# Loading the overflow flag before the last expert and closing a trunk kernel inside the branch

## The chip, the cores and the metric

The kernel runs on one core of one Trainium2 chip. The time is device microseconds of that core for one execution of the whole program. The four computing engines and the queues are called PE (matrix products; PEld is its weight load), DVE (vector), ACT (scalar activations), POOL (GpSimd) and SP (which issues the DMAs). Each runs its own instruction stream, and they meet only at semaphores.

## The reference, cut to what matters

Two layers over 256 tokens of width 1024 (4 tiles of 128x512 hold the residual stream). The part that this text is about is the second half of layer 1 and the last line:

```python
# layer 1: top-2-of-8 experts, each a SwiGLU of width 3584, then the final norm
logits = h @ w_router                       # 256 x 8
gates  = softmax(top2(logits))
for e in range(8):                          # only the tokens that chose e
    x[tok_e] += gate_e * ((silu(h[tok_e] @ w_gate[e]) * (h[tok_e] @ w_up[e])) @ w_down[e])
out = x * rsqrt(mean(x * x, axis=-1) + 1e-6) * final_norm
```

Layer 0 (dilated window attention and a dense SwiGLU) and the pooling mixer of layer 1 come before it and are the same in both kernels.

## The kernel before, in words

The tokens sit in `x` as two tiles `t` of 128 rows, each read in two column halves `n` of 512. Weights arrive from memory in units of 1 MB (128x2048 float32). ACT copies each unit to a rounded form `w_hi` (line 338), DVE subtracts it to get the rest `w_lo` (line 343), and PE forms three products per pair of operands (lines 375 to 377). At most three units are split ahead of PE, so ACT may split unit u+3 only when PE has finished unit u.

The experts run in a loop that each engine executes in its own stream: `Fori(0, 7)` holds seven experts, and the eighth, "the last expert", is written out once behind the loop, because it needs no next expert prepared. The tokens of an expert fit in 128 slots in the usual case. If one expert is chosen by more than 128 tokens, a second round over all eight experts is needed. Whether it is, stands in one integer in SBUF, `over_i` (the overflow flag), which DVE writes before the first expert. Each engine reads it into a register (`value_load`), compares and branches with `If(more != 0)`; behind it, in the usual case, an `Else` branch that is empty. The second round lies in the instruction stream between the branch and what follows.

Where the reading stands matters here. ACT and DVE first wait until the last piece of the last expert has been added to `x` (semaphore `x_added`, line 961 adds four pieces, in the order of `SCATTER`), then read the flag (lines 662 and 989), then branch (lines 663 and 990). Then the final norm: ACT sums the squares of tile 0 (line 475) and DVE those of tile 1 (line 681), DVE forms the mean (688), ACT the root (479), DVE the reciprocal (693), and DVE forms the four output pieces of 128x512 (line 1004). SP, which has read the flag and branched much earlier (lines 420, 421), stores each piece when it is ready (line 430) and waits until the stores have landed; then all engines meet in a closing barrier (line 154). PE reads and branches at lines 1343 and 1344.

Of the kernel before, what the change touches and what calls it, by code (L numbers as in the profile page):

```python
# [5 lines left out]
ALU = mybir.AluOpType  # L21
ACT = mybir.ActivationFunctionType
# [19 lines left out]
E = 8  # L42
# [106 lines left out]
def program(nc, x_in, ffn_norm, w_qkv, w_o, pool_w, pool_scale, w_gate, w_up, w_down,  # L149
# [4 lines left out]
    with ctx:  # L154
        def sb(name, shape, dt=F32, scope=ctx):
            return scope.enter_context(nc.sbuf_tensor(name, shape, dt))

        def sem(name):
            return ctx.enter_context(nc.semaphore(name))
# [28 lines left out]
        over_i = sb("over_i", [P, 1], I32)  # L188

# [94 lines left out]
        y_hi_ready, y_lo_ready = sem("y_hi_ready"), sem("y_lo_ready")  # L284
        scatter_ready, x_added, out_stored = sem("scatter_ready"), sem("x_added"), sem("out_stored")
# [100 lines left out]
        def _(sp):  # L386
# [34 lines left out]
            with sp.If(more != 0):  # L421
                with sp.Fori(0, E) as e:
                    expert(e + E, e)
            with sp.Else():
                sp.nop()
            for q in range(2 * TT):
                t, n = q // 2, q % 2
                cols = slice(n * 512, (n + 1) * 512)
                sp.wait_ge(hn_ready, TT + q + 1)
                sp.dma_start(out[t * P:(t + 1) * P, cols], hn[:, t, cols]).then_inc(out_stored, 16)  # L430
            sp.wait_ge(out_stored, 16 * 2 * TT)
# [35 lines left out]
        def _(act):  # L467
# [192 lines left out]
            round_of_experts(0)  # L660
            act.wait_ge(routed, 1)
            more = act.value_load(over_i[0:1, 0:1], min_val=0, max_val=1)
            with act.If(more != 0):
# [4 lines left out]
                act.nop()  # L668
            with act.Else():
                act.nop()  # L670
            squares(4)
            root(4)
# [3 lines left out]
        def _(dve):  # L676
# [289 lines left out]
            def round_of_experts(first):  # L966
# [10 lines left out]
                with dve.Fori(0, E - 1) as e:  # L977
                    expert(e + first, first, False)
                expert(first + E - 1, first, True)
                dve.wait_ge(x_added, START + 4 * (first + E))  # L980

# [6 lines left out]
            round_of_experts(0)  # L988
            more = dve.value_load(over_i[0:1, 0:1], min_val=0, max_val=1)
            with dve.If(more != 0):  # L990
# [4 lines left out]
                dve.nop()  # L995
            with dve.Else():
                dve.nop()
            squares(4)
            mean(4)
            invert(4)  # L1000
            for t in range(TT):
                for n in range(2):
                    cols = slice(n * 512, (n + 1) * 512)
                    nc.vector.scalar_tensor_tensor(hn[:, t, cols], x[:, t, cols], rstd(4, t), rows[:, 2, cols],
                                                   ALU.mult, ALU.mult).then_inc(hn_ready, 1)
# [406 lines left out]
```

## Time and profile before

| what | us |
|---|---|
| median of 3 runs | 1588.21 |
| lowest and highest | 1586.06 and 1589.52 |
| profiled execution: span | 1587.4 |
| busy: PE, DVE, ACT | 1540.5, 1233.1, 971.2 |
| last addition of the last expert ends | 1575.97 |
| first output piece starts | 1582.11 |

The profile is of one further execution; its own time is given by its span, from its first to its last instruction, and no figure is listed for what lies around the span. The span lies between the lowest and the highest of the runs. A busy share tells which engine carries the long stretches; the end of the program has to be read in the chain and the timeline, since nearly all engines are idle there.

### The profile page before, as it was taken

The page shows a single profiled execution, that of the slowest core. Times are in us where ns is not written, and L with a number is a line of the kernel's source. Part 1 is how long each engine was busy: PE and PEld are TensorE (multiplying, and loading weights), DVE is VectorE, ACT ScalarE, POOL GpSimd, SP SyncE. Part 2 cuts the span into 40 slices and gives each one's busy share as a digit, 9 for nine tenths or more (in the row PEclk, how much of TensorE's full clock was granted, in tenths as well). Part 3 has the DMA queues.
Part 4 walks back from the last instruction along what each step waited for, and adds up shares of the span by engine and source line. Part 5 has one row for each costly group of instructions (what it writes and reads, how often), then busy time and mean ns, then how long its engine had stood idle before and what let it go on. Part 6 is the DMA issues. An engine that isn't in the chain of part 4 may idle for free.

```text
span 1587.4 us, 22195 instructions
## 1 busy us (share of the span) xinstructions
PE 1540.5 (97%) x8546; PEld 1323.0 (83%) x8546; DVE 1233.1 (78%) x999; ACT 971.2 (61%) x797; POOL 89.9 (6%) x50
## 2 busy tenths in 40 slices
PE   6999999999999699999999999999999999999996
PEld 6999999899998688888888888888888888888885
DVE  6877667664445768888888888888888888888886
ACT  4344444454334457777777777777777777776774
POOL 1333223000000100000000000000000000000000
PEclk9999999999999689999999999999999999999998
DMA  9644443355557379999999999999999999999980
GB/s 310 201 146 133 134 153 127 94 186 186 183 182 246 132 264 341 355 342 342 361 340 358 338 347 362 337 360 336 339 358 347 334 359 345 341 362 341 357 301 28
DMA packets 217117, 436.80 MB, mean 275 GB/s; under 512 B 6992, under 2 KB 68176, under 8 KB 217056
## 3 DMA queue, kind: packets, MB, share of 16 engines
q1 hardware_dynamic: 215168, 432.11, 77.1%
q10 hardware_dynamic: 1552, 2.77, 0.5%
q0 software_dynamic: 336, 1.09, 0.2%
q8 instruction: 42, 0.69, 0.2%
q14 instruction: 19, 0.16, 0.0%
HBM read 434.88 MB, written 1.05 MB: 275 GB/s over the span
## 4 chain that ended last, share of the span: by engine, by line
PE 94%; DVE 4%; issue 1%; ACT 1%; DMA 0%; DVEq 0%; ACTq 0%; SPq 0%
PE bank L375 28%; PE bank L377 28%; PE bank L376 28%; PE bank L1249 2%; PE bank L1122 2%; PE bank L1259 2%; PE bank L1109 1%; PE bank L1099 1%; DVE w_lo L343 1%; DVE rot L764 1%; PE bank L1321 0%; PE bank L1322 0%; PE bank L1015 0%; DMA x<-in_x 0%; PE bank L1142 0%
## 5 line engine op out<-in xcount | busy, mean ns | idle before, releaser
L343 DVE TENSOR_TENSOR w_lo<-raw,w_hi 128x2048 fp32r<-128x2048 f32 x202 | 462.9, 2294 | 158.5 <-ACT w_hi L338 156.8
L338 ACT ACTIVATE w_hi<-raw 128x2048 fp32r<-128x2048 f32 x202 | 386.4, 1914 | 157.7 <-PE bank L377 154.6
L375 PE MATMUL bank<-w_hi,xg_hi 128*128 128x512 f32 x896 | 361.1, 403 | 0.0
L376 PE MATMUL bank<-w_lo,xg_hi 128*128 128x512 f32 x896 | 356.0, 397 | 0.0
L377 PE MATMUL bank<-w_hi,xg_lo 128*128 128x512 f32 x896 | 356.0, 397 | 0.0
L343 DVE TENSOR_TENSOR w_lo<-raw_late,w_hi 128x2048 fp32r<-128x2048 f32 x95 | 217.8, 2292 | 48.2 <-ACT w_hi L338 47.0
L343 DVE TENSOR_TENSOR w_lo<-raw_more,w_hi 128x2048 fp32r<-128x2048 f32 x96 | 220.0, 2291 | 29.6 <-ACT w_hi L338 28.9
L338 ACT ACTIVATE w_hi<-raw_more 128x2048 fp32r<-128x2048 f32 x96 | 184.0, 1917 | 55.7 <-PE bank L377 55.7
L377 PEld LDWEIGHTS bank<-w_hi,xg_lo 128*128 128x128 f32 x896 | 169.2, 189 | 41.3
L376 PEld LDWEIGHTS bank<-w_lo,xg_hi 128*128 128x128 f32 x896 | 169.7, 189 | 38.6
L375 PEld LDWEIGHTS bank<-w_hi,xg_hi 128*128 128x128 f32 x896 | 169.5, 189 | 38.7
L338 ACT ACTIVATE w_hi<-raw_late 128x2048 fp32r<-128x2048 f32 x95 | 181.7, 1913 | 31.9 <-PE bank L377 31.9
L375 PE MATMUL bank<-w_hi,a_hi 128*128 128x256 f32 (+1 forms) x592 | 174.2, 294 | 1.2 <-DVE rot L764 0.9
L377 PE MATMUL bank<-w_hi,a_lo 128*128 128x256 f32 (+1 forms) x592 | 171.0, 289 | 0.0
L376 PE MATMUL bank<-w_lo,a_hi 128*128 128x256 f32 (+1 forms) x592 | 170.9, 289 | 0.0
L375 PE MATMUL bank<-w_hi,hT_hi 128*128 128x512 f32 x384 | 152.8, 398 | 0.0
L376 PE MATMUL bank<-w_lo,hT_hi 128*128 128x512 f32 x384 | 152.2, 396 | 0.0
L377 PE MATMUL bank<-w_hi,hT_lo 128*128 128x512 f32 x384 | 152.2, 396 | 0.0
L375 PE MATMUL bank<-a_hi,w_hi 128*128 128x256 f32 x384 | 111.5, 290 | 5.7 <-DVE w_lo L343 5.7
L375 PEld LDWEIGHTS bank<-w_hi,a_hi 128*128 128x128 f32 x592 | 113.3, 191 | 3.7 <-issue 1.0
L377 PEld LDWEIGHTS bank<-w_hi,a_lo 128*128 128x128 f32 x592 | 113.4, 192 | 1.4
L376 PEld LDWEIGHTS bank<-w_lo,a_hi 128*128 128x128 f32 x592 | 113.5, 192 | 0.8
(158 smaller groups left out, 1991.0 us busy)
## 6 DMA issues: line engine op xcount, KB each, us to landing
raw_more<-in_moe_w_gate SPq DMA_DIRECT2D x48, 1024.0 KB, 5.5
raw<-in_moe_w_gate SPq DMA_DIRECT2D x48, 1024.0 KB, 5.4
raw_late<-in_moe_w_down SPq DMA_DIRECT2D x48, 1024.0 KB, 5.2
raw<-in_moe_w_up SPq DMA_DIRECT2D x40, 1024.0 KB, 5.5
raw_late<-in_moe_w_up SPq DMA_DIRECT2D x40, 1024.0 KB, 5.2
raw<-in_moe_w_down SPq DMA_DIRECT2D x40, 1024.0 KB, 5.1
raw<-in_attn_w_qkv SPq DMA_DIRECT2D x36, 1024.0 KB, 5.1
raw_more<-in_moe_w_up SPq DMA_DIRECT2D x32, 1024.0 KB, 5.7
```

Source lines behind the costliest of these rows:

```text
L338: nc.scalar.activation(w_hi[:, u % SPLIT, :], where, ACT.Copy).then_inc(hi_ready, 1)
L343: nc.vector.tensor_tensor(w_lo[:, u % SPLIT, :], home(u, i)[0], w_hi[:, u % SPLIT, :].bitcast(F32), ALU.subtract).then_inc(lo_ready, 1)
L375: nc.tensor.matmul(bank, hi, w[0], start=start, stop=False)
L376: nc.tensor.matmul(bank, hi, w[1], start=False, stop=False)
L377: return nc.tensor.matmul(bank, lo, w[0], start=False, stop=stop)
L764: last = nc.vector.tensor_tensor(turned[to:to + h2], bank[of:of + h2], sin[of:of + h2, :].unsqueeze(1).to_broadcast([h2, 2, SEQ]), ALU.mult)
L1099: last = nc.tensor.matmul(ps[3 + side][:, at:at + kn], qkT[part, c % 2, 0, g, pair, t * P:(t + 1) * P], qkT[part, c % 2, 1, g, pair, k0:k0 ...
L1109: last = nc.tensor.transpose(ps[5 + side][:, k * P:(k + 1) * P], e_sb[:, side, k * P:(k + 1) * P], ident[:, :])
L1122: last = nc.tensor.matmul(ps[7][:, side * HD:(side + 1) * HD], eT[:, side, k * P:(k + 1) * P], v_sb[:, c % 2, g, kt, col:col + HD], start= ...
L1249: last = nc.tensor.matmul(bank[:, q * P:(q + 1) * P], src[:, c:c + P], pick[:, t, :], start=t == 0, stop=t == TT - 1)
L1259: last = nc.tensor.transpose(ps[6][:, q * P:(q + 1) * P], h[:, q * P:(q + 1) * P], ident[:, :])
```

## The change

Three of the five streams change behind the loop of experts (PE only in the numbers of its lines; POOL not at all).

1. ACT and DVE read the overflow flag between the loop and the last expert. SP reads it where it did.
2. The comparison is turned round, `If(more == 0)`: the usual case is now the code directly behind the branch, and the second round is in the `Else`. The closing work (`finish`, and on SP `store_output`) is written out in both branches, so that in the usual case each of the three engines leaves the branch by a jump over the second round to the closing barrier.
3. The squares are all summed on ACT, in four pieces of 128x512, each as soon as its addition is done. The root-mean factor is formed from the four sums.
4. Tile 1 of the output is formed in two steps: DVE multiplies `x` by the gain row while ACT still sums squares, and ACT scales that by the reciprocal root. Tile 0 is formed by DVE as before. SP stores tile 0's two pieces, then tile 1's.

```diff
+            def store_output():
+                for t, ready in ((0, hn_ready), (1, out_ready)):
+                    for n in range(2):
+                        sp.wait_ge(ready, (TT if t == 0 else 0) + n + 1)
+                        sp.dma_start(out[t * P:(t + 1) * P, cols], hn[:, t, cols]).then_inc(out_stored, 16)
+                sp.wait_ge(out_stored, 16 * 2 * TT)
+
+            with sp.If(more == 0):
+                store_output()
+            with sp.Else():
                 with sp.Fori(0, E) as e:
                     expert(e + E, e)
-            with sp.Else():
-                sp.nop()
...
                 with act.Fori(0, E - 1) as e:
                     expert(e + first, False)
+                more = None
+                if not first:
+                    act.wait_ge(routed, 1)
+                    more = act.value_load(over_i[0:1, 0:1], min_val=0, max_val=1)
                 expert(first + E - 1, True)
                 load_table(ACT.Sqrt, 2 if first else 0)
-                act.wait_ge(x_added, START + 4 * (first + E))
...
+            def finish(first):                      # ACT
+                junk = (hn[:, 0, 0:512], sg[:, :], hn[:, 0, 512:D], h[:, :])
+                for q, (n, t, _bank) in enumerate(SCATTER):
+                    act.wait_ge(x_added, START + 4 * (first + E - 1) + q + 1)
+                    nc.scalar.activation(junk[q], x[:, t, n * 512:(n + 1) * 512], ACT.Square, scale=D ** -0.5,
+                                         accum_out=ssq[:, n, t:t + 1]).then_inc(ssq_ready, 1)
+                root(4)
+                act.wait_ge(rstd_ready, 5)
+                for n in range(2):
+                    act.wait_ge(weighted_ready, n + 1)
+                    nc.scalar.activation(hn[:, 1, cols], hn[:, 1, cols], ACT.Copy, scale=rstd(4, 1)).then_inc(out_ready, 1)
...
+            def finish(first):                      # DVE
                 dve.wait_ge(x_added, START + 4 * (first + E))
+                for n in range(2):
+                    nc.vector.tensor_tensor(hn[:, 1, cols], x[:, 1, cols], rows[:, 2, cols], ALU.mult).then_inc(weighted_ready, 1)
+                dve.wait_ge(ssq_ready, 4)
+                nc.vector.scalar_tensor_tensor(stat[:, 4, 2:2 + TT], ssq[:, 0, :], EPS, ssq[:, 1, :], ALU.add, ALU.add)
+                invert(4)
+                for n in range(2):
+                    nc.vector.scalar_tensor_tensor(hn[:, 0, cols], x[:, 0, cols], rstd(4, 0), rows[:, 2, cols],
+                                                   ALU.mult, ALU.mult).then_inc(hn_ready, 1)
```

What DVE holds from the last expert's additions on. Before, the flag's load and the branch follow the additions, and the second round (from the third row on from the branch) lies between the branch and the norm:

```order
499 L961 SCALAR_TENSOR_TENSOR x<-bank,gate_w,x 128x512 x4
500 L989 TENSOR_LOAD over_i
501 L989 ISA x2
502 L990 COMPARE_AND_BRANCH
503 L343 TENSOR_TENSOR w_lo<-raw_more,w_hi 128x2048 x3
...
677 L996 UNCONDITIONAL_BRANCH
678 L681 ISA hn,stat<-x 128x1024
679 L681 ISA stat 128x1
680 L688 TENSOR_SCALAR stat<-stat 128x2
681 L693 RECIPROCAL stat<-stat 128x2
682 L1004 SCALAR_TENSOR_TENSOR hn<-x,stat,rows 128x512 x4
```

The same place of DVE in the changed kernel, beginning with the loop's own branch (460):

```order
460 L981 COMPARE_AND_BRANCH
461 L986 TENSOR_LOAD over_i
462 L986 ISA x2
463 L330 TENSOR_TENSOR w_lo<-raw,w_hi 128x2048 x3
...
501 L965 SCALAR_TENSOR_TENSOR x<-bank,gate_w,x 128x512 x4
502 L1012 COMPARE_AND_BRANCH
503 L995 TENSOR_TENSOR hn<-x,rows 128x512 x2
504 L997 SCALAR_TENSOR_TENSOR stat<-ssq 128x2
505 L697 RECIPROCAL stat<-stat 128x2
506 L1002 SCALAR_TENSOR_TENSOR hn<-x,stat,rows 128x512 x2
507 L1012 UNCONDITIONAL_BRANCH
508 L330 TENSOR_TENSOR w_lo<-raw_more,w_hi 128x2048 x3
```

The load went from behind the additions to in front of the last expert's first own split; the norm stands directly behind the branch; and a jump (507) follows the norm, over the second round. ACT's stream changes in the same way.

SP around its branch and at its end, before; row 297 stores the four output pieces, row 298 waits for their landing:

```order
179 L420 TENSOR_LOAD over_i
180 L420 ISA x2
181 L421 COMPARE_AND_BRANCH
182 L422 UNCONDITIONAL_BRANCH
...
296 L424 UNCONDITIONAL_BRANCH
297 L430 DMA out<-hn 128x512 x4
298 L154 UNCONDITIONAL_BRANCH
```

SP now:

```order
181 L416 COMPARE_AND_BRANCH
182 L413 DMA out<-hn 128x512 x4
183 L416 UNCONDITIONAL_BRANCH
184 L419 UNCONDITIONAL_BRANCH
...
297 L413 DMA out<-hn 128x512 x4
298 L418 UNCONDITIONAL_BRANCH
```

The jump over the second round's DMAs stood ahead of the stores (181 to 297) and now stands behind them (183 to behind 298); it is row 183 that waits for the landing.

## Rows read from the trace of the kernel before

**Rows 1.** The page: span, busy time by engine, shares of the chain that ended last.
```profile
span 1587.4 us, 22195 instructions
PE 1540.5 (97%) x8546; PEld 1323.0 (83%) x8546; DVE 1233.1 (78%) x999; ACT 971.2 (61%) x797; POOL 89.9 (6%) x50
PE 94%; DVE 4%; issue 1%; ACT 1%; DMA 0%; DVEq 0%; ACTq 0%; SPq 0%
```

**Rows 2.** The chain in order of time from 1570: start us, us, what.
```profile
1573.24 2.74 DVE x L961 x4
1575.97 0.03 issue
1576.00 0.55 DVEq L989
...
1576.91 0.06 DVEq L990
1576.97 3.23 issue
1580.21 0.58 DVE hn L681
...
1582.11 0.75 DVE hn L1004
```

**Rows 3.** Lines 662, 663, 1344: durations ns min/median/max, first and last start.
```profile
L662 ACTq TENSOR_LOAD <-over_i x1: 488/488/488, 1576.0 to 1576.0; - x1
L663 ACTq COMPARE_BRANCH  x1: 54/54/54, 1576.8 to 1576.8; - x1
L1344 PEldq COMPARE_BRANCH  x1: 3654/3654/3654, 1574.0 to 1574.0; - x1
```

**Rows 4.** Timeline from 1576: start us, us, engine, instruction, [idle before].
```profile
1579.58 1.06 ACT L475 ACTIVATE hn<-x 128x1024 f32<-128x1024 f32 x1 [5.73 <-issue]
1581.47 0.17 DVE L688 TENSOR_SCALAR stat<-stat 128x2 f32<-128x2 f32 x1
1582.11 2.74 DVE L1004 SCALAR_TENSOR_TENSOR hn<-x,stat,rows 128x512 f32<-128x512 f32 x4
1582.89 2.32 SPq L430 DMA_DIRECT2D out<-hn  x4
```

**Rows 5.** DVE and ACT at the start of the last expert, and one PE instruction.
```profile
1451.79 2.28 DVE L343 TENSOR_TENSOR w_lo<-raw_more,w_hi 128x2048 fp32r<-128x2048 f32 x1
1455.24 2.29 DVE L343 TENSOR_TENSOR w_lo<-raw,w_hi 128x2048 fp32r<-128x2048 f32 x1 [1.17 <-ACT w_hi L338]
...
1453.29 1.92 ACT L338 ACTIVATE w_hi<-raw 128x2048 fp32r<-128x2048 f32 x1 [3.15 <-PE bank L377]
...
1458.89 0.39 PE L376 MATMUL bank<-w_lo,xg_hi 128*128 128x512 f32 x1
```

**Rows 6.** Groups of instructions from 528 to 560; then ACT's timeline from 235.
```profile
L869 DVE TENSOR_TENSOR x<-x,hn 128x512 f32<-128x512 f32 x4 | 2.8, 692 | 0.1
...
235.53 0.72 ACT L540 ACTIVATE e_sb<-s_sb,softs 128x512 f32<-128x512 f32 x1 [3.56 <-DVE softs L783]
236.16 0.18 ACT L540 ACTIVATION_READ_ACCUMULATOR e_sb<-s_sb,softs 128x1 f32 x1
236.39 0.72 ACT L540 ACTIVATE e_sb<-s_sb,softs 128x512 f32<-128x512 f32 x1
```

**Rows 7.** DMA from 1582 to 1588 by queue; line 430's landing; SP's first issues.
```profile
q1 hardware_dynamic: 576, 1.05, 47.0%
...
DMA to landing us min/median/max: 2.1/2.1/2.1
...
0.75 0.40 SPq L391 DMA_DIRECT2D ident<-in_ident_in  x1
1.20 0.43 SPq L392 DMA_DIRECT2D x<-in_x  x1
```

**Rows 8.** DMA queues (packets, MB, share) in 1576.9:1578.4, then in 1540.7:1543.4, then line 421.
```profile
q8 instruction: 1, 0.02, 5.0%
q14 instruction: 2, 0.02, 2.6%
...
q1 hardware_dynamic: 229, 0.94, 89.7%
...
L421 SPq COMPARE_BRANCH  x1: 50/50/50, 1540.6 to 1540.6; - x1
```

**Rows 9.** SP's line 417 from 1412 to 1414, and line 154 from 1586 to 1588.
```profile
L417 SPq COMPARE_BRANCH  x1: 45/45/45, 1413.0 to 1413.0; - x1
L417 SPq FUSED_REGOPS  x1: 50/50/50, 1413.3 to 1413.3; - x1
...
L154 SPq COMPARE_BRANCH  x1: 38/38/38, 1587.0 to 1587.0; - x1
L154 SPq DRAIN  x1: 13/13/13, 1587.2 to 1587.2; - x1
```

More of the change, by code:

```diff
@@ L188, in program @@
         over_i = sb("over_i", [P, 1], I32)
+        ssq = sb("ssq", [P, 2, TT])
         attn = ExitStack()
@@ L284, in program @@
         y_hi_ready, y_lo_ready = sem("y_hi_ready"), sem("y_lo_ready")
+        ssq_ready, weighted_ready, out_ready = sem("ssq_ready"), sem("weighted_ready"), sem("out_ready")
         scatter_ready, x_added, out_stored = sem("scatter_ready"), sem("x_added"), sem("out_stored")
@@ L420, in _ @@
             more = sp.value_load(over_i[0:1, 0:1], min_val=0, max_val=1)
-            with sp.If(more != 0):
+            def store_output():
+                for t, ready in ((0, hn_ready), (1, out_ready)):
+                    for n in range(2):
+                        cols = slice(n * 512, (n + 1) * 512)
+                        sp.wait_ge(ready, (TT if t == 0 else 0) + n + 1)
[4 more added lines that the diff above has]
+            with sp.Else():
                 with sp.Fori(0, E) as e:
                     expert(e + E, e)
-            with sp.Else():
-                sp.nop()
[L426 to L431, printed above, removed]
+                store_output()
         @block.gpsimd
@@ L667, in _ @@
                 round_of_experts(E)
[L668 to L672, printed above, removed]
+                finish(E)
         @block.vector
@@ L978, in round_of_experts @@
                     expert(e + first, first, False)
+                more = None
+                if not first:
+                    dve.wait_ge(routed, 1)
+                    more = dve.value_load(over_i[0:1, 0:1], min_val=0, max_val=1)
                 expert(first + E - 1, first, True)
+                return more
+            def finish(first):
                 dve.wait_ge(x_added, START + 4 * (first + E))
+                for n in range(2):
+                    cols = slice(n * 512, (n + 1) * 512)
+                    nc.vector.tensor_tensor(hn[:, 1, cols], x[:, 1, cols], rows[:, 2, cols], ALU.mult).then_inc(weighted_ready, 1)
+                dve.wait_ge(ssq_ready, 4)
+                nc.vector.scalar_tensor_tensor(stat[:, 4, 2:2 + TT], ssq[:, 0, :], EPS, ssq[:, 1, :], ALU.add, ALU.add)\
+                    .then_inc(var_ready, 1)
+                invert(4)
+                for n in range(2):
+                    cols = slice(n * 512, (n + 1) * 512)
+                    nc.vector.scalar_tensor_tensor(hn[:, 0, cols], x[:, 0, cols], rstd(4, 0), rows[:, 2, cols],
+                                                   ALU.mult, ALU.mult).then_inc(hn_ready, 1)
             for counter in (h_ready, hT_lo_ready, x_added, y_lo_ready):
@@ L987, in _ @@
             nc.vector.tensor_reduce(over[:, 0:1], far, AX.XY, ALU.add).then_inc(over_ready, 1)
-            round_of_experts(0)
-            more = dve.value_load(over_i[0:1, 0:1], min_val=0, max_val=1)
-            with dve.If(more != 0):
+            more = round_of_experts(0)
+            with dve.If(more == 0):
+                finish(0)
+            with dve.Else():
                 split_lo(dve, U_MOE + E * UE)
@@ L994, in _ @@
                 round_of_experts(E)
[L995 to L1005, printed above, removed]
+                finish(E)
         @block.tensor
```

10 lines of the change are left out of this document (6 added, 4 removed).

## The prediction, made before the changed kernel ran

> **What bounds the kernel now.** I read the page first. PE is busy for 97% of the span, and the chain that ended last is 94% PE [rows 1]. None of PE's work is touched, so up to the last expert's result the time can only stay or grow. The change acts where PE is done. So I read next the chain in order of time over the last 17 us. The reader is to see three stretches. The last four additions of the last expert take DVE from 1573.24 to 1575.97. From there until the first output piece starts at 1582.11 there are 6.14 us, and more than half of that is no work at all: the flag is loaded (0.55 us, with some register work up to 1576.91), a branch of 0.06 us, and then 3.23 us "issue" before the sums of squares begin [rows 2]. ACT shows the same: load 0.49 us, branch 0.05 us at 1576.8, and its first instruction at 1579.58 [rows 3, 4], about 2.75 us after the branch. The third stretch is output and store: 1582.11 to the landing of the last piece, then the closing barrier, end at 1587.4.
>
> Last I asked what the 3.23 us are. In the 1.5 us after the branches the DMA view lists two packets of queue 14 and one of queue 8, all of the kind "instruction" [rows 8]: the code behind a taken far branch is fetched, and the engine waits. PE pays 3.65 us for its own branch, which is off the path since PE is done [rows 3].
>
> **The load of the flag ahead of the last expert.** On the path it removes 0.94 us of DVE (1575.97 to 1576.91) [rows 2]. It adds the same 0.9 us to DVE and to ACT at the start of the last expert. Queued behind it is the split of the next weight unit. DVE's current split ends at 1454.07 and its next starts at 1455.24 after 1.17 us idle; ACT idles 3.15 us before its own at 1453.29 [rows 5]. Even if the load had to wait until DVE is empty, it would end at 1454.07 + 0.94 = 1455.01, ahead of 1455.24. Behind that there is a second cover: this split ends at 1457.53, and PE reads such a low half next at 1458.89 [rows 5], 1.3 us later. Cost 0. Bounds: 0, and 3.2 us of stall (if a fetch like that of rows 2 came with it on a drained DVE: 1455.01 + 3.23 is 3.0 late, less 1.3 cover, 1.7 us on PE, so 1.7 and not 3.2). I take 0, because the load is short and the two covers together are 1.5 us beyond it.
>
> **The usual case straight on.** Removes the 3.23 us of DVE, and ACT's 2.75 beside it. What replaces it is an untaken branch, 0.06 us, which is passed while the additions still run, since nothing ahead of it waits for them. Between 0 and 3.23 us could remain, should the code straight on not be there either; I take 0, since the gap is seen behind taken branches, and of the whole chain, nearly all of it straight code, only 1% is issue [rows 1].
>
> **Squares by pieces.** Before, from 1580.21 to the mean at 1581.47 are 1.26 us of path. Now ACT sums piece by piece from about 1574.05 (first addition done at 1573.99). No row shows a Square of 128x512 from SBUF; the nearest is the Exp with a sum: 0.72 us, its accumulator read 0.63 after the start, the next start after 0.86 us [rows 6]. By that the fourth piece starts at max(1575.97 + 0.06, 1574.05 + 3 x 0.86) = 1576.63 and its sum is there at 1577.44. From below: the 128x1024 Square took 1.06 us [rows 4], half its columns cannot take less than half of it, so 1576.03 + 0.53 + 0.18 = 1576.74. DVE meanwhile multiplies tile 1 by the gain row, two instructions like L869, 0.69 us each [rows 6], from 1576.00, to between 1577.30 (overlapped starts, as L1004's four take 2.74 and not 3.0) and 1577.38. So the tiny addition that replaces the mean starts at 1577.3 to 1577.45. I take 1577.33: late next is DVE's own product, ACT's last sum is about level with it. From there mean, root, reciprocal cost what they cost now, 1581.47 to 1582.11 = 0.64 us [rows 4, 2]. First output piece at 1577.97 instead of 1582.11: **4.14 us less**.
>
> **The final product on two engines.** DVE does two pieces of 0.75 instead of four; ACT scales the other two beside it (about 0.72 each by the row nearest, done near 1578.7 and 1579.4). That looks like 1.3 us gained, since DVE's four take 2.74 [rows 4]. I count it at nothing, for the store. The stores move 1.05 MB, and their packets fill all 16 DMA engines for 47.0% of a window of 6 us, 2.8 us [rows 7]; four pieces spaced 0.66 us apart is just that rate. The DMA engines are thus busy without a break from the first piece on, and pieces that are ready sooner only queue. What a store needs is set by the first issue: 1582.89, and the last landing is 2.1 us after the last issue at about 1584.88, so 4.1 us after the first. Now: first issue 1577.97 + 0.78 = 1578.75, last landing 1582.87. Bounds of the gain: 0, and 0.4 us (issues at 1578.75, 1579.4, then SP's own rate of 0.45 us [rows 7], last one 1580.3 + 2.1 = 1582.4). I take 0, because the busy time is the nearer row.
>
> **The exits.** The jump over the second round has not gone; it has moved behind `finish`. On DVE and ACT it may be taken when the last instruction is handed to the engine, at about 1578.0 and 1578.7. With 3.23 and 2.75 us they reach the barrier at 1581.4, ahead of the stores' landing at 1582.9. Covered by 1.4 us, cost 0; without that cover it would be the whole 3 us. On SP nothing covers it: the jump itself waits for the landing. Before, SP's last branch ran to its neighbour: 1587.0, and DRAIN at 1587.2 [rows 9]. Now it passes 115 listed rows. What that costs lies between a jump whose target is at hand (the loop's back edge, branch at 1413.0 and next instruction at 1413.3, 0.2 us more than nothing [rows 9]) and PE's 3.65 us [rows 3]. The choice rests on a jump of nearly the same length that SP took before, at 1540.6: in the 2.7 us after it there is no packet of an instruction queue [rows 8], while the two engines that stalled had theirs within 1.5 us. So SP's target was at hand, and I take +0.1 us.
>
> The page "Runtime: NRT & Kernel Launch" of the Trainium skill, section "Instruction fetch mechanics", says that an engine holds two lines of 16 KiB (256 instructions) and that a taken branch out of this window must fetch before going on. It speaks against this change as far as it goes: the far jump is paid wherever it stands, and SP's is now last. The trace agrees that a far jump fetches. Of the size it shows packets of 8 KB on queue 14 (two of them make 0.02 MB [rows 8]). By lines of 256, SP's 115 rows would mostly stay inside the window; by lines of half that they may reach the second next.
>
> **The sum.** -4.14 (first output piece) + 0 (store) + 0.1 (SP's exit) = -4.0 us against the profiled execution: span 1583.4. That execution is 0.8 us under the median of the runs; what lies around the span I leave as it is, so the median goes from 1588.2 to **1584.2**.
>
> **Rivals.**
> SP's exit is fetched. For: the code behind it was never run, and if SP keeps only the next line, the last store's wait stands at another place in it. Against: rows 8. It gives 2.75 to 3.65 us more, less the 0.1: 1586.9 to 1587.8, about 1587.3.
> The exit costs more than the whole gain (the slower side). Place: SP between the last landing and the barrier. If SP had to wait for two lines one after the other, 2 x 3.23 = 6.5 us, the result is 1584.2 + 6.4 = 1590.6. It decides from the point where the jump costs over 4.1 us; the dearest seen is 3.65.
> The start of the last expert loses. ACT or DVE held there for 3 us and more, PE stalls 1 to 2 us: 1585.2 to 1586.2. Against: rows 5.
> The store is not bound by transfer, the shared product pays: 1583.8.
> The change does not do what it says, the code straight on stalls as well: the 3.23 us stay and only load and squares gain, 1587.4.
>
> **How the numbers follow.** Forecast 0.68; SP's exit fetched 0.13; straight-on stall 0.04; loss at the last expert 0.05; shared product pays 0.06; slower 0.04. A difference of under 0.2% (3.2 us) cannot be told from none here; the runs before lie 3.5 us apart. The forecast's own range, 1583.2 to 1585.3, is narrow, but a median of few runs moves by about 1 us, and so of the forecast some 0.57 of 0.68 ends beyond 3.2 us, with the shared product's 0.06 and a little of the third rival: faster 0.64. Slower 0.04, the rest 0.32. Range 1582.2 to 1587.4: it takes in the third rival and most of the first.
>
> **What would show it right or wrong.** Right: ACT's first Square before 1575; DVE's product at 1576.0 after the last addition, no "issue" over 0.1 us there; first output piece 2.0 us after the last addition (before, 6.1); first issue to last landing still 4.1 us; on SP 0.2 to 0.4 us between the branch that waits for the stores and DRAIN; DVE and ACT at their DRAIN more than a microsecond before SP. All times shift if PE ends elsewhere; the stretch from the last addition to the end, 11.4 us before, should be 7.4. Wrong: this stretch is 10 us or more, with an instruction packet after SP's last branch; DVE's idle time at the start of the last expert gone and PE waiting for `w_lo`; a store shorter than 3.8 us.

## The result: 0.56% faster, by twice the forecast, and mostly where nothing was expected

| kernel | median us (lowest to highest, 4 runs) | profiled span | up to the last addition | last addition to end |
|---|---|---|---|---|
| before | 1588.26 (1586.06 to 1589.52) | 1587.4 | 1575.97 | 11.4 |
| after | 1579.47 (1578.85 to 1579.62) | 1577.5 | 1568.04 | 9.5 |

The ratio after to before is 0.9944, 95% interval 0.9932 to 0.9957: 8.8 us less. The forecast was 1584.2 with a range down to 1582.2, so the result lies outside. The two profiled spans differ by 9.9 us. Of these, 7.9 us were gained before the last addition of the last expert, where the forecast had nothing, and only 1.9 of the 4.0 forecast behind it.

The page of the kernel after: span, busy time by engine, shares of the chain that ended last, answering [rows 1].

```profile
span 1577.5 us, 22202 instructions
PE 1532.5 (97%) x8546; PEld 1322.7 (84%) x8546; DVE 1231.1 (78%) x997; ACT 974.0 (62%) x805; POOL 89.9 (6%) x50
PE 94%; DVE 4%; ACT 1%; issue 1%; DMA 0%; ACTq 0%; SPq 0%; DVEq 0%
```

PE runs the same 8546 products and is busy 8.0 us less (1540.5 before). So the same products go faster. The windows view shows it in a stretch of 500 us that lies wholly in the loop of experts. The columns are: stretch, its length, busy us and count of instructions of PE, PEld, DVE, ACT and POOL, granted clock, DMA share, GB/s. First before, then after:

```profile
900.00:1400.00 500.00, 500.00 (x2269) 406.00 (x2268) 432.18 (x261) 360.38 (x250) 0.00 (x0) 1.00 0.96 347
```

```profile
900.00:1400.00 500.00, 500.00 (x2281) 408.89 (x2280) 435.06 (x263) 362.56 (x250) 0.00 (x0) 1.00 0.96 350
```

PE is busy without a gap in both, at a granted clock of 1.00 (the upper level, 2.4 GHz) in both, and starts 2281 instructions instead of 2269. Neither a wait nor the clock differs in this stretch. PE's own loop branch gives the time of one expert (line, operation, durations in ns, first and last start of seven). Before, then after:

```profile
L1336 PEldq COMPARE_BRANCH  x7: 76/208/232, 688.1 to 1448.4; - x7
```

```profile
L1350 PEldq COMPARE_BRANCH  x7: 76/208/228, 686.2 to 1441.3; - x7
```

Six experts take 760.3 us before and 755.1 after: 126.7 and 125.9 us each. The 7.9 us are 1.9 up to the first of these branches, 5.2 over the six experts and 0.8 behind: within the experts the gain grows evenly with the products.

Of the first 1.9 us, about 0.5 is not the products' rate but lies at the start: at 33 us the same DVE instruction starts 0.45 us sooner, and at 300 us it is still 0.50. What the rows show there is the granted clock. PE is at the lower level (1.2 GHz) from 13.3 to 20.1 us in the profiled execution of before, and has no such stretch in that of after. Before, then after:

```profile
0.00:100.00 100.00, 86.18 (x687) 84.66 (x688) 71.33 (x85) 44.15 (x48) 28.19 (x29) 0.97 0.71 234
```

```profile
0.00:100.00 100.00, 86.14 (x691) 84.59 (x692) 71.35 (x85) 44.04 (x48) 28.18 (x29) 1.00 0.71 236
```

The stretch at the end, as the chain in order of time (start us, us, what), of the kernel after, answering [rows 2]:

```profile
1567.28 0.75 DVE x L965
1568.04 0.02 issue
1568.06 1.29 DVE hn L995 x2
1569.35 0.08 DVE stat L997
...
1569.69 0.18 DVE stat L697
1569.87 0.02 issue
1569.89 0.06 DVE hn L1002
...
1570.56 0.75 DVE hn L1002
```

The 3.23 us "issue" are gone, no "issue" above 0.02 us stands between the last addition and the first piece, and that piece starts 1.86 us after the addition's end instead of 6.14. ACT's timeline shows the squares by pieces (start us, us, instruction, idle before):

```profile
1566.08 0.63 ACT L659 ACTIVATE hn<-x 128x512 f32<-128x512 f32 x1 [0.18 <-DVE x L965]
...
1566.74 0.63 ACT L659 ACTIVATE sg<-x 128x512 f32<-128x512 f32 x1
...
1568.06 0.63 ACT L659 ACTIVATE h<-x 128x512 f32<-128x512 f32 x1
```

Then the store. SP's line 413, the four stores of the output (durations of the issues in ns, first and last start), and their landing:

```profile
L413 SPq DMA_DIRECT2D out<-hn x4: 369/444/1247, 1570.7 to 1573.1; - x4
...
DMA to landing us min/median/max: 2.8/2.9/3.7
```

From the first issue at 1570.7 to the last landing (1573.1 + 3.7) are 6.1 us; before, 4.1 [rows 4, 7]. One issue took 1.25 us, where they take about 0.4 otherwise. The DMA queues (packets, MB, share of the 16 engines) between 1570.4 and 1572.2, in that issue's time:

```profile
q1 hardware_dynamic: 106, 0.22, 36.2%
q14 instruction: 3, 0.02, 7.1%
q8 instruction: 1, 0.02, 4.8%
```

Code is being fetched while the output is stored. Last, the closing barrier, line 139: DVE and ACT reach it at 1573.4 and 1573.6, 3.7 us and more ahead of SP, whose last branch (it ends the wait for the landing) starts at 1576.8.

```profile
L139 DVEq DRAIN  x1: 58/58/58, 1573.4 to 1573.4; - x1
L139 ACTq DRAIN  x1: 81/81/81, 1573.6 to 1573.6; - x1
L139 SPq DRAIN  x1: 49/49/49, 1577.3 to 1577.3; - x1
```

Their own jumps over the second round (the last of two branches each, DVE's and ACT's) start at 1569.9, so from jump to barrier each takes 3.5 to 3.7 us, across the whole first part of the store:

```profile
L1012 DVEq COMPARE_BRANCH  x2: 43/45/47, 1566.7 to 1569.9; - x2
L669 ACTq COMPARE_BRANCH  x2: 38/41/44, 1563.8 to 1569.9; - x2
```

### The profile page after: what moved, and what is told of

The parts are those of the page before. It is cut to its first block, busy times and chain, and to the rows that moved or that the text cites. A ratio compares the mean times of both kernels' runs of the same rounds, so it can differ in the third digit from the quotient of the medians.

```text
span 1577.5 us, 22202 instructions
## 1 busy us (share of the span) xinstructions
PE 1532.5 (97%) x8546; PEld 1322.7 (84%) x8546; DVE 1231.1 (78%) x997; ACT 974.0 (62%) x805; POOL 89.9 (6%) x50
## 4 chain that ended last, share of the span: by engine, by line
PE 94%; DVE 4%; ACT 1%; issue 1%; DMA 0%; ACTq 0%; SPq 0%; DVEq 0%
PE bank L362 28%; PE bank L364 28%; PE bank L363 28%; PE bank L1263 2%; PE bank L1136 2%; PE bank L1273 2%; PE bank L1123 1%; PE bank L1113 1%; DVE w_lo L330 1%; DVE rot L768 1%; PE bank L1335 0%; PE bank L1336 0%; PE bank L1029 0%; DMA x<-in_x 0%; PE bank L1156 0%
```

## The experiments

Times are medians; each kernel is compared with runs of the kernel before on the same chip. Two questions: why PE got faster, and where 2 us of the end went.

### Where PE's 7.9 us come from: the place of the tiles

**The padding alone, and the change without the shift.** The first kernel is the kernel before with 32 unused bytes, the second the changed one with `ssq` allocated last.

```diff
         over_i = sb("over_i", [P, 1], I32)
+        pad = sb("pad", [P, 8])                  # e1_pad_all, on the kernel before
...
-        ssq = sb("ssq", [P, 2, TT])              # e2_change_no_shift, on the kernel after
...
         place = sb("place", [P, SEQ], F32R)
+        ssq = sb("ssq", [P, 2, TT])
```

> The kernel before with an unused tile of 32 bytes per partition put where the change put its new tile ssq; no instruction differs. Theory A (addresses): what the change gained before the last expert, 7.9 us, comes from the tiles allocated behind the new one, which move from 32 to 0 modulo 64 bytes. Then this kernel gains 7.4 to 8.0 us on the kernel before, and the product of 512 columns starts every 232.5 ns instead of 234.2. Theory B (code): the gain comes from what the change does to the instruction streams. Then this kernel is level with the kernel before, within 1 us.

> The changed kernel with its new tile ssq allocated last, so that every other tile has the address it had before. Theory A: the 7.9 us are gone and only the end of the program is faster, by 2.0 us as the two traces show: 1.6 to 2.4 us under the kernel before. Theory B: 9 to 10 us under it, as the changed kernel.

Measured: the padding alone 1580.83, ratio 0.9956 (0.9940 to 0.9973), 7.4 us less. The change without the shift 1586.62, ratio 0.9991 (0.9982 to 1.0001), 1.6 us less, which the interval just doesn't set apart from no change. PE's loop branch, first with the padding, then with the change but not the shift:

```profile
L1337 PEldq COMPARE_BRANCH  x7: 76/208/227, 686.5 to 1441.6; - x7
```

```profile
L1350 PEldq COMPARE_BRANCH  x7: 76/208/232, 687.4 to 1447.7; - x7
```

That is 125.9 and 126.7 us for an expert: the first is the kernel after, the second the kernel before. The shift is enough and it is needed; 7.4 and 1.6 make 9.0, about the 8.8 us of both. The theory holds and the rival falls. Which property of the place counts is the next question.

**Which tiles.** Padding ahead of `router_sb` moves the gathered tokens (`xg`) and `hT` and all behind, but not the dense layer's `dhT`. The next moves the landing buffers and the dense layer's tiles to 0 past a multiple of 128, and the experts' to 32. The third moves `xg` alone. The fourth moves everything behind `over_i` by 64 bytes, from 96 to 32.

```diff
+        pad = sb("pad", [P, 8])                   # e3_pad_gathered
         router_sb = sb("router_sb", [P, KD, E])
...
         over_i = sb("over_i", [P, 1], I32)
+        pad = sb("pad", [P, 8])                   # e4_pad_landing
...
+        pad_back = sb("pad_back", [P, 8])
         y_hi = sb("y_hi", [P, D], F32R)
...
+        pad = sb("pad", [P, 8])                   # e12_pad_xg_only
         xg_hi = sb("xg_hi", [P, KD, P], F32R)
         xg_lo = sb("xg_lo", [P, KD, P], F32R)
+        pad_back = sb("pad_back", [P, 24])
...
+        pad = sb("pad", [P, 16])                  # e10_pad_64, behind over_i
```

> The kernel before with the unused 32 bytes further on, behind the landing tiles raw_more and raw_late: only the router's tiles, xg_hi, xg_lo, sg, h, hT_hi, hT_lo, pick and place move. Theory A1 (the matrices that PE loads as weights must start at a multiple of 64 bytes): the experts' gain comes back nearly whole, 6.5 to 7.3 us; the rest (dense layer, and the last of seven down blocks, whose hidden tile lies in y_hi) does not. Theory A2 (the tiles that DMAs land in): no gain, within 1 us.

> The kernel before with 32 unused bytes ahead of raw_more and 32 more ahead of y_hi: the landing tiles and the dense layer's tiles move to a multiple of 64, and everything from y_hi on stays off it. Theory A1: the experts' gain does not come, at most the dense layer's 0.4 us: within 1 us of the kernel before. Theory A2: 6.5 to 7.5 us faster.

> The kernel before, in which only xg_hi and xg_lo move from 96 to 0 modulo 128 bytes; a second unused tile puts everything behind them back. Theory A1 (what counts is where the matrix lies that PE loads as weights): the three products per weight pair with xg take 703.2 ns together as in the changed kernel (707.8 before), and the three with hT stay at 704.3 ns (698.3 in the changed kernel). That is 42 units x 8 experts x 2/3 x 4 x 4.6 ns = 4.1 us faster. Rival A3 (what counts is one of the tiles beside them, sg, h, pick or place): no gain, within 1 us.

> The kernel before with 64 unused bytes where the change put 32: every tile behind goes from 96 to 32 modulo 128, and stays 32 modulo 64. Theory A1 with a step of 64: no gain, within 1 us. Theory A1 with a finer dependence, modulo 128 (the run with the landing tiles moved had its weights at 32 modulo 128 and gained 3.4 us, which was not expected): about that gain, 3 to 4 us. Theory A2 (the landing tiles had that gain): none.

The table has, beside the time, what PE needs for the three products of a pair of operands, in ns: the mean from the start of one product to the start of the next in the trace (gaps of 0.4 us and more left out), summed over the three, for those that load `xg`, `hT` and (dense layer) `dhT`. In brackets the distance: the loaded tile's address less the streamed one's, modulo 128 bytes.

| kernel | median us | against before | xg | hT | dhT |
|---|---|---|---|---|---|
| before | 1588.3 | | 707.8 [96] | 704.3 [96] | 703.1 [96] |
| after | 1579.5 | -8.8 | 703.2 [0] | 698.3 [0] | 698.4 [0] |
| e3_pad_gathered | 1579.9 | -8.3 | 703.1 [0] | 698.2 [0] | 703.2 [96] |
| e4_pad_landing | 1584.9 | -3.4 | 705.4 [32] | 701.6 [32] | 698.4 [0] |
| e12_pad_xg_only | 1583.2 | -5.5 | 702.8 [0] | 701.1 [96] | 703.2 [96] |
| e10_pad_64 | 1585.0 | -3.7 | 705.4 [32] | 701.6 [32] | 700.8 [32] |

The rates are the surer columns, since the medians also hold what the clock did. The five runs of e3 lie at 1579.7 to 1579.9 (three) and at 1583.0 (two). The profiled one is of the first kind; PE has a granted clock of 0.85 there between 500 and 600 us, against 0.81 in the profiled execution of before. So part of its 8.3 us is the clock's: the ratio over all its runs (0.9960, 0.9946 to 0.9975) makes 6.4 us, near the 6.9 that the rates give (896 x 4.7 and 448 x 6.1 ns).

A tile's products change with that tile's place and not with the landing buffers': in e3 the dense layer stays at its old rate and the experts take the new one. I had missed that e4 would gain (it was expected to stay within 1 us): a distance of 32 is also better than 96. In e12 `hT` did not move, yet its products take 701.1 and not 704.3, so a tile's own distance is not the whole of it; that I can't explain. For the kernel after the rates account for 896 x 4.6 ns = 4.1 us (`xg`), 448 x 6.0 = 2.7 (`hT`) and 88 x 4.7 = 0.4 (`dhT`): 7.2 of 7.9 us. With the 0.5 us from the first 33 us, nearly all is accounted for.

**Is it the address or the distance, and is 0 best?** These start from the kernel after: everything behind `ssq` 64 bytes on; `w_hi` and `w_lo` at 32 and everything behind them at 64; only `w_hi` and `w_lo` at 64, the rest at 0; everything behind `w_lo` at 64.

```diff
         ssq = sb("ssq", [P, 2, TT])
+        pad = sb("pad", [P, 16])                  # e11_change_plus_64
...
+        pad_w = sb("pad_w", [P, 8])               # e5_shift_w; e14_w_64 has [P, 16]
         w_hi = sb("w_hi", [P, SPLIT, UNIT], F32R)
         w_lo = sb("w_lo", [P, SPLIT, UNIT], F32R)
+        pad_w_back = sb("pad_w_back", [P, 8])     # e14_w_64 has [P, 16]
         a_hi = sb("a_hi", [P, KD * SEQ], F32R)
...
+        pad = sb("pad", [P, 16])                  # e15_a_64, behind w_lo
```

> The changed kernel with 64 unused bytes more, so that every tile behind over_i lies at 64 modulo 128 instead of 0. Step of 64: level with the changed kernel, 1579 to 1580.5. Step of 128: slower by some microseconds.

> The changed kernel with the streamed weights w_hi and w_lo moved from 0 to 32 modulo 128 and everything behind them to 64. In the experts these two tiles are what PE streams past, not what it loads; in the attention's queries and keys they are what it loads (256 columns streamed). If only the loaded matrix counts: the experts keep 703.2 and 698.3 ns per three products (unless 64 modulo 128 is worse than 0, which the run beside this one tells), and only the query and key products could change. If any operand counts: the experts lose the 4.6 ns again, 7 us.

> The changed kernel with only w_hi and w_lo moved, from 0 to 64 modulo 128; all the rest stays at 0. Theory A4 (what counts is the distance between the matrix that PE loads and the columns that it streams, modulo 128: so far 96 gave 707.8 ns per three xg products, 32 gave 705.4, 0 gave 703.2, 64 gave 692.8): 692.8 and 688.6 ns as with 64 the other way round, and a time of 1562 to 1565. Rival A1 (the loaded matrix's own place counts): 703.2 and 698.3 ns in the experts, 1579 to 1580.5.

> The changed kernel with everything from a_hi on moved to 64 modulo 128, w_hi and w_lo left at 0. Theory A4 (distance): the experts 692.8 and 688.6 ns per three products; the query and key products (w loaded, a streamed) 372.5 ns and the 256-column products with a loaded 363.3 ns per three, as when w was the one moved; about 6 to 9 us under the kernel with only the tiles behind over_i at 64, so 1555 to 1558. If a tile's own place counts: the 256-column products stay at 382.9 and 370 ns, 1563 to 1564.

| kernel | median us | ratio (95%) | xg | hT | dhT | a loaded, w streamed | w loaded, a streamed |
|---|---|---|---|---|---|---|---|
| after | 1579.5 | 0.9944 (0.9932 to 0.9957) | 703.2 [0] | 698.3 [0] | 698.4 [0] | 382.9 [0] | 368.7 [0] |
| e11_change_plus_64 | 1563.5 | 0.9846 (0.9829 to 0.9862) | 692.8 [64] | 688.6 [64] | 688.2 [64] | 382.9 [0] | 371.8 [0] |
| e5_shift_w | 1576.5 | 0.9923 (0.9907 to 0.9940) | 705.2 [32] | 701.7 [32] | 700.6 [32] | 379.6 [32] | 359.7 [96] |
| e14_w_64 | 1556.6 | 0.9800 (0.9784 to 0.9817) | 693.2 [64] | 688.9 [64] | 699.1 [64] | 372.5 [64] | 357.1 [64] |
| e15_a_64 | 1556.3 | 0.9802 (0.9785 to 0.9820) | 693.2 [64] | 688.9 [64] | 699.1 [64] | 373.7 [64] | 355.5 [64] |

The last two columns are products of 256 columns in the parts ahead of the experts: with `a` loaded those of the values and of the dense layer, with `w` loaded those of the queries and keys. The text on record ahead of e15 has these two kinds the wrong way round. Its 363.3 is for `w` loaded, with the stretch at 1.2 GHz at 14 to 21 us in it; outside it e14 takes 357.1. PE's loop branch of e11, then the window of 500 us:

```profile
L1351 PEldq COMPARE_BRANCH  x7: 76/208/228, 681.7 to 1426.7; - x7
```

```profile
900.00:1400.00 500.00, 500.00 (x2313) 413.30 (x2312) 439.88 (x267) 367.45 (x254) 0.00 (x0) 1.00 0.97 356
```

The loop branch of e14, then of e15:

```profile
L1352 PEldq COMPARE_BRANCH  x7: 76/208/232, 674.5 to 1419.8; - x7
```

```profile
L1351 PEldq COMPARE_BRANCH  x7: 76/208/237, 674.4 to 1419.7; - x7
```

An expert takes 124.2 us in all three, again with PE busy for the whole window and the clock at 1.00. I had expected e11 level or slower; it gained 25 us on the kernel before and 16 on the kernel after, more than anything the change was written for. Two more forecasts missed. e5 was to leave the experts alone or cost 7 us, and came out 3.0 us under the kernel after: the experts lost a little, the 256-column products gained more. e14 was to end at 1562 to 1565 and ended at 1556.6, for the same reason. e14 and e15 place different tiles at 64 (the streamed in one, the loaded in the other) and agree to 0.1 us for the experts: for `xg` and `hT` what counts is the distance between the two, not the address of either. e5 says the same at 32: `xg` at 64 with `w` at 32 goes like `xg` at 32 with `w` at 0 in e10 (705.2 and 705.4). For the 512-column products with `xg` and `hT`, 96 is slowest, then 32, then 0, and 64 is fastest. Two things don't fit a single rule. The 256-column products order the distances differently: with `w` loaded, 96 takes 359.7, nearly as little as 64, and 0 is the slowest of each kind. Small differences mean little there, since at the same distance of 0 the queries and keys take 365.0 in the kernel before and 371.8 in e11. And `dhT` at distance 64 takes 688.2 in e11 but 699.1 in e14 and e15, so something besides the distance of the two tiles has a part in it; what, no run shows.

### Where 2 us of the end went: the jumps out of the branch

The stretch from the last addition to the end was forecast at 7.4 us and took 9.5. The last column of the table below carries this part; the medians also hold how long PE stood at the lower clock between 500 and 600 us. My theory was that the jumps of ACT and DVE over the second round fetch code while the output is stored, and so slow it down; the rivals were SP's own jump, and the two engines' pieces ready too close together.

**The exits taken away, or turned round.** The first kernel has no branch and no second round on ACT and DVE; it leaves out the second round there, which these inputs don't need. The second branches on ACT and DVE right behind the load of the flag, with the last expert written in both branches, and the usual case in the `Else` that runs on into the barrier; SP branches and stores as in the kernel before. The third is the kernel after with only SP's part as before.

```diff
-            with act.If(more == 0):               # e6_exits_gone; DVE alike
-                finish(0)
-            with act.Else():
-                ...
+            finish(0)
...
-            with act.If(more == 0):               # e7_branch_early; DVE alike
-                finish(0)
+            with act.If(more != 0):               # last_of: expert(first + E - 1), the table's load
+                last_of(0)
                 ...
+            with act.Else():
+                last_of(0)
+                finish(0)
...
-            with sp.If(more == 0):                # e7_branch_early and e8_sp_before
-                store_output()
-            with sp.Else():
+            with sp.If(more != 0):
                 with sp.Fori(0, E) as e:
                     expert(e + E, e)
-                store_output()
+            with sp.Else():
+                sp.nop()
+            store_output()
```

> The changed kernel without the branch and the second round on ACT and DVE (the round is left out, which these inputs do not need; SP and PE keep theirs). In the changed kernel the stores take 6.1 us from the first issue to the last landing instead of 4.1, and SP's second issue 1.25 us instead of 0.36, while three instruction packets go at 1570.5 to 1572. Theory C (the code fetched for DVE's and ACT's exits gets in the way of the stores): 4.1 us again, the end 7.3 to 7.7 us after the last addition instead of 9.5, about 2 us under the changed kernel's 1579.5. Rival D (stores are slow because of the pieces that ACT forms, or because of SP's own place in the code): still 6 us.

> ACT and DVE branch right behind the flag's load, ahead of the last expert, which stands in both branches; the usual case is the Else, which runs on to the barrier without another jump. SP branches and stores as before the change, behind the If. Theory C: fetches of 2.75 and 3.23 us fall at the start of the last expert, where ACT has 3.15 us and DVE about 3.3 us (its load ended at 1444.9, its next split starts at 1448.14): 0 to 0.5 us of stall for PE. The stores take 4.1 us, SP's exit 0.15 instead of 0.49: end 7.0 to 7.4 us after the last addition, 1577.2 to 1577.8. If a far branch there does hold up the splits: PE idle at the start of the last expert, and 1578.5 or more.

> The changed kernel with SP's branch and stores as before the change (branch over the second round, then the stores, no jump behind them); ACT and DVE as in the changed kernel. If SP's exit costs 0.35 us and its place has nothing to do with the slow stores: from the last landing to SP's DRAIN 0.15 us instead of 0.5, stores still 6 us, end 9.1 to 9.2 us after the last addition. If the stores are slow because of SP: 4.1 us, and the end 7.1 us after it.

| kernel | median us | first issue to last landing | last landing to DRAIN | last addition to end |
|---|---|---|---|---|
| after | 1579.5 | 6.1 | 0.50 | 9.5 |
| e6_exits_gone | 1577.5 | 4.6 | 0.51 | 8.0 |
| e7_branch_early | 1577.5 | 4.1 | 0.18 | 7.2 |
| e8_sp_before | 1578.2 | 6.0 | 0.18 | 9.0 |

Line 413 of e6, then of e7:

```profile
L413 SPq DMA_DIRECT2D out<-hn x4: 368/440/877, 1570.6 to 1572.6; - x4
...
DMA to landing us min/median/max: 2.4/2.6/2.6
```

```profile
L413 SPq DMA_DIRECT2D out<-hn x4: 356/405/453, 1571.0 to 1572.5; - x4
...
DMA to landing us min/median/max: 2.1/2.2/2.5
```

In e7 no issue takes longer than 0.45 us, the landing is back at 2.2 us, and the store at the 4.1 us of before. In e6, where I had expected 4.1 us and an end at 7.3 to 7.7, one issue still takes 0.88 us; there one packet of queue 14 and one of queue 8 fall into the store, at 1570.6 and 1570.7, where e7 has none and the kernel after has three of queue 14 in its first issues. With SP's part undone but the exits in place, the store keeps its 6.0 us. So the exits of ACT and DVE cost the store 1.5 us (e6), though both engines were at the barrier long before SP. The other 0.5 us goes together with the last two packets, in e7; whose code they hold is not shown. SP's jump costs 0.3 us. The products shared by two engines gain nothing: in e7, as forecast, the store takes as long as before though its pieces are ready sooner. How a fetch holds up SP's issue is not shown.

e7 pays elsewhere. DVE's timeline at the start of its last expert:

```profile
1449.38 4.50 DVE L330 TENSOR_TENSOR w_lo<-raw,w_hi 128x2048 fp32r<-128x2048 f32 x2 [2.76 <-issue]
```

The waits there (engine, line, waited for: us, times, longest):

```profile
DVE w_lo L330 <- issue: 2.8, 1, 2.8
...
PE bank L362 <- DVE w_lo L330: 0.4, 1, 0.4
```

The taken branch now stalls DVE by 2.8 us in the middle of the work (and ACT by 3.7), and PE by 0.4 us.

**The flag's load, and the wait behind the branch.** The kernel before, with the load moved on ACT and DVE, and with it the wait for the last addition, which stood ahead of the load and now stands behind the branch, as in the kernel after (DVE's part; ACT's is alike):

```diff
                 with dve.Fori(0, E - 1) as e:
                     expert(e + first, first, False)
+                more = None
+                if not first:
+                    dve.wait_ge(routed, 1)
+                    more = dve.value_load(over_i[0:1, 0:1], min_val=0, max_val=1)
                 expert(first + E - 1, first, True)
-                dve.wait_ge(x_added, START + 4 * (first + E))
...
-            more = dve.value_load(over_i[0:1, 0:1], min_val=0, max_val=1)
...
+            dve.wait_ge(x_added, START + 4 * E)
             squares(4)
```

> The kernel before with the flag's load alone moved ahead of the last expert; branch, norm and addresses as before. The branch can now be taken when the last addition has been handed to DVE, 1.3 us before it ends, so its 3.23 us end 1.9 us after it, and the sums of squares start there instead of 4.2 us after it: 2.3 us under the kernel before, end 8.9 to 9.2 us after the last addition. If the branch waits until the additions are done: 0.9 us under it.

Measured 1586.52, ratio 0.9986 (0.9977 to 0.9996), and 9.0 us from the last addition to the end (8.9 to 9.2 expected). DVE's branch, and the timeline there:

```profile
L996 DVEq COMPARE_BRANCH  x1: 63/63/63, 1573.7 to 1573.7; - x1
...
1575.07 1.06 ACT L475 ACTIVATE hn<-x 128x1024 f32<-128x1024 f32 x1 [2.15 <-DVE x L964]
...
1576.82 1.23 DVE L684 CUSTOM_DVE_ANT_0 hn<-x 128x1024 f32<-128x1024 f32 x1 [1.78 <-issue]
```

With the register ready and no wait ahead of it, DVE's branch is taken at 1573.7, 1.3 us before the last addition ends, and the fetch lies beside the additions: ACT waits for nothing but the addition, DVE for 1.78 us instead of 3.23 and the load. The code of the norm is otherwise that of before, no exit stands behind it, and the store takes its 4.1 us. This stretch ends 0.5 us sooner than in the kernel after: the other three parts together gain 1.8 us up to the first piece (3.69 after the addition here, 1.86 there) and lose 2.3 behind it, in the store and in SP's exit.

### Both together

The two placings with a distance of 64, and the branch ahead of the last expert (the edits of e15 and of e14, each with that of e7):

> The placing of the run beside this one together with the branch of ACT and DVE ahead of the last expert and SP's branch ahead of its stores. If the two gains add: 2 us under the run beside this one. If the faster PE leaves ACT and DVE no slack for the fetch at the start of the last expert: PE stalls there 1 us or more and 1 us or less is left.

> The placing with only w_hi and w_lo at 64 (1556.6 in its own run) together with the early branch: 1554.2 to 1555 if the gains add, 1555.6 or more if PE stalls at the start of the last expert.

Measured 1556.37, ratio 0.9804 (0.9787 to 0.9820), and 1555.76, ratio 0.9795 (0.9779 to 0.9811). The 2 us hoped for from the branch did not show: e15 and e14 can't be told from them. The end takes 7.2 us as it should. The waits of e16 between 1420 and 1452 show what it costs:

```profile
DVE w_lo L332 <- issue: 3.7, 1, 3.7
PEld bank L364 <- DVE w_lo L332: 1.9, 1, 1.9
PE bank L364 <- DVE w_lo L332: 1.5, 1, 1.5
```

With PE faster, DVE and ACT have less spare time at that place, and the stall of DVE reaches PE with 1.5 us instead of 0.4. The best kernels are about 1556 us, 2.0% below before; the branching makes no difference that was measured.

## Why the prediction was wrong, step by step

**"None of PE's work is touched, so up to the last expert's result the time can only stay or grow."** This step failed, and it is most of the miss: 7.9 us, of which 7.2 follow from the products' rates and 0.5 go with the clock in the first 33 us. The work is the same, its operands' places are not. The diff shows `ssq` among the allocations of the kernel after; a list of the tiles' addresses beside it would have shown the rest, though nothing in the trace of before tells what a place is worth. With the shift taken out, the kernel lies at 1586.62, inside the range, but near its slow end and by two misses: the start came out as forecast, and the exits took back half of it.

**The flag's load, cost 0.** Right. The rows of the kernel after at the start of the last expert, DVE's then ACT's, answering [rows 5]:

```profile
1448.14 2.29 DVE L330 TENSOR_TENSOR w_lo<-raw,w_hi 128x2048 fp32r<-128x2048 f32 x1 [1.15 <-ACT w_hi L325]
...
1446.19 1.92 ACT L325 ACTIVATE w_hi<-raw 128x2048 fp32r<-128x2048 f32 x1 [3.13 <-PE bank L364]
```

The idle times are those of before, 1.15 and 3.13 us, and DVE still waits for ACT. The load vanished in them. Moved together with the wait for the additions, it is worth more than the 0.94 us given to it: e9 gained 2.5 us in the last stretch (11.4 to 9.0), since the fetch can then start beside the additions. I had credited that to the turned branch.

**The usual case straight on: no stall.** Right, 0.02 us.

**Squares by pieces; first piece 2.0 us after the last addition, 4.14 sooner.** Right: 1.86 us, 4.28 sooner. A Square of 128x512 takes 0.63 us and the next starts 0.66 later, less than the 0.72 and 0.86 taken from the Exp; as foreseen the path ran over DVE's own two products.

**The shared product, 0.** Right, by e7.

**Exits of DVE and ACT, "Covered by 1.4 us, cost 0".** This term failed too. It is at least the 1.5 us that e6 gives back, and 2.0 us with the packets that only e7 is rid of. The two engines did reach the barrier early, 3.7 us and more ahead of SP, though each took 3.5 to 3.7 us from its jump and not the 2.75 and 3.23 reckoned. I asked only whether they arrive in time and not what their fetches do to the store that runs meanwhile, which [rows 8] would have let me ask: they show the packets of such a fetch. The page "Runtime: NRT & Kernel Launch" of the Trainium skill, section "Instruction fetch mechanics", says that a taken branch out of the window forces a DMA fetch; the packets agree. It names the stall of the engine that jumps, and here the cost that counted was on another, which the page does not speak of.

**SP's exit, 0.1 us.** Nearly: 0.3 us (0.50 from the last landing to DRAIN, where e8 has 0.18). Neither the rival at 1587 nor the slower one came about.

The sum of the last stretch: -4.3 (first piece) + 2.0 (store) + 0.3 (SP's exit) = -2.0, or -1.9 before rounding, against -4.0 forecast; with -7.9 ahead of it, -9.9 us of the two spans.

## What to carry to other kernels

A new tile, however small, moves the tiles allocated behind it; before an edit is given credit or blame, compare the addresses, or run the old code with the same padding. Where matrix products fill the time, try the distance between the loaded and the streamed operand modulo 128 bytes: it took some 30 of 1588 us here, and all the rest of the change 1.6. A branch whose register is loaded early and that has no wait ahead of it lets part of its fetch run beside the work before it. And a far jump moved to the end can cost whoever uses the DMA engines then, even if the engine that jumps has nothing left to do: here 1.5 us or more of the store.

## What was new of the hardware

- A 512-column product in this kernel starts every 235.9, 235.1, 234.4 or 230.9 ns (a third of 707.8, 705.4, 703.2 and 692.8) for a distance of 96, 32, 0 or 64 bytes modulo 128 between the loaded and the streamed tile, with `xg` loaded. The page "TensorE: Matmul & The Clock Gate" of the Trainium skill, section "Step-by-step: what each phase is for", says that the engine has two independent read ports, so that loading weights takes nothing from the product that runs. The page says nothing of addresses; taken alone, it leaves no place for such a difference. The runs show one, and the measurement decides. What in the engine or the memory makes the difference is not shown.
- The four stores of the output took 6.1 us instead of 4.1 while code was fetched, and a single issue on SP 1.25 us instead of 0.4. In the seven kept traces with both exits (after, e2, e5, e8, e11, e14, e15) the second issue takes 1.15 to 1.54 us, in the three with the early branch (e7, e13, e16) 0.36 to 0.48.
- A fetch behind a far branch that is taken early overlaps with the work already handed to the engine: 1.78 us of DVE's stall remained of 3.23 (e9).
